# Turned tables in another order, a pooling weight and table copies begun elsewhere, and bias rows multiplied on TensorE, in a hybrid SSM and mixture-of-experts block

## The reference

```
mod = silu(c) @ w_mod + b_mod                       # six rows of 1024: shift, scale, gate, twice
hx  = rmsnorm(x, g_mix) * (1 + sc1) + sh1           # the same for ctx, with c_ctx's rows
ux  = hx @ w_in;   uc_ssm = hc @ w_in[:, 512:]
ssm  = S5 scan both ways (32 groups of 16 channels, 64 complex states), started from ctx's last state;
       gelu, then y * sigmoid(y @ w_glu + b_glu)
pool = (centred mean over 2/4/8/16 - u) @ w_pool[g] * s_pool      # four groups of 128 channels
x   = x + g1 * (concat(pool, ssm) @ w_out)
h2  = rmsnorm(x, g_ffn) * (1 + sc2) + sh2
experts, gates = group-limited top 2 of 32 by sigmoid(h2 @ w_router)
x   = x + g2 * sum(gate_e * (silu(h2 @ w_gate[e]) * (h2 @ w_up[e])) @ w_down[e])
out = rmsnorm(x, g_final)
```

## Time and profile before

| | |
|---|---|
| median of three runs | 665.77 us (665.63 to 666.22) |
| the profiled execution | 667.83 us |
| its span, first to last instruction | 665.7 us |
| busy in the span: TensorE / weight loads | 586.6 us (88%) / 248.5 us (37%) |
| busy: DVE / ScalarE / POOL | 201.5 (30%) / 149.4 (22%) / 57.5 us (9%) |
| moved by DMA | 248.99 MB, mean 374 GB/s |

### The profile page before, as it was taken

One profiled execution on the slowest core, in us unless ns is written; L12 is line 12 of the kernel. 1 busy time (PEld: TensorE's weight loads), 2 busy tenths in 40 slices (PEclk: granted clock), 3 DMA queues, 4 the chain that ended last, 5 costly groups with the idle time before them and its releaser, 6 DMA issues.

```text
span 665.7 us, 9385 instructions
## 1 busy us (share of the span) xinstructions
PE 586.6 (88%) x3770; PEld 248.5 (37%) x3770; DVE 201.5 (30%) x427; ACT 149.4 (22%) x239; POOL 57.5 (9%) x103
## 2 busy tenths in 40 slices
PE   1989995799789997899799979978997997899996
PEld 0454552465453333234233323423342342234331
DVE  7999388769850010002001000200110010002003
ACT  8472131031322212012111211221022112012111
POOL 4993000011300000000000000000000000000000
...
GB/s 314 421 401 89 253 244 333 292 412 389 378 278 420 423 420 422 422 421 423 420 423 419 422 421 422 423 420 423 422 423 420 423 421 421 423 421 366 402 207 64
DMA packets 47463, 248.99 MB, mean 374 GB/s; under 512 B 8888, under 2 KB 11592, under 8 KB 21072
## 3 DMA queue, kind: packets, MB, share of 16 engines
...
q0 software_dynamic: 352, 1.07, 0.7%
...
## 4 chain that ended last, share of the span: by engine, by line
PE 64%; DMA 24%; DVE 7%; issue 2%; ACT 1%; SPq 1%; DVEq 0%; POOL 0%; ACTq 0%
PE ps L847 21%; DMA wts<-in_w_up 21%; PE ps L887 17%; PE ps L817 5%; PE ps L823 5%; PE ps L609 4%; DVE rc L1168 3%; PE ps L699 2%; PE ps L622 2%; DMA ra<-in_w_pool 2%; DMA cb<-in_ssm_bc 1%; PE ps L642 1%; DVE ps L1168 1%; PE ps L512 1%; PE ps L863 1%
## 5 line engine op out<-in xcount | busy, mean ns | idle before, releaser
L847 PE MATMUL ps<-wts,ra 128*64 128x512 f32 x512 | 239.3, 619 | 36.1 <-DMA wts<-in_w_up 36.1
L848 PE MATMUL ps<-wts,ra 128*64 128x512 f32 x512 | 239.4, 620 | 0.0
L847 PEld LDWEIGHTS ps<-wts,ra 128*64 128x64 f32 x512 | 69.2, 142 | 179.5 <-issue 128.5
L887 PE MATMUL ps<-wts,ra 128*32 128x512 f32 x512 | 111.4, 593 | 0.0
L887 PE MATMUL ps<-rc,ra 128*32 128x512 f32 x512 | 111.4, 593 | 0.0
L1168 DVE TENSOR_TENSOR ra<-ra,ps 128x256 f32<-128x256 f32 x32 | 13.5, 422 | 270.6 <-ACT ra L1117 270.4
L1111 ACT COPY ra<-ps 128x512 f32<-128x512 f32 x32 | 33.5, 1048 | 211.6 <-PE ps L848 211.6
L848 PEld LDWEIGHTS ps<-wts,ra 128*64 128x64 f32 x512 | 69.2, 142 | 0.0
L887 PEld LDWEIGHTS ps<-wts,ra 128*32 128x32 f32 x512 | 29.2, 110 | 73.2 <-issue 73.2
L1168 DVE TENSOR_TENSOR cb<-ps,ra 128x512 f32<-128x512 f32 x32 | 22.2, 692 | 103.4 <-PE ps L887 103.4
L1106 ACT COPY ra<-ps 128x512 f32<-128x512 f32 x32 | 18.7, 585 | 140.8 <-PE ps L817 140.8
...
## 6 DMA issues: line engine op xcount, KB each, us to landing
...
```

The source lines that it names most:

```text
L847: pe.matmul(ps[0:64, 4 + b, :], st, Wg[b][:, k, :], start=(k == 0), stop=(k == KD - 1))
L848: mm = pe.matmul(ps[64:128, 4 + b, :], st, Wu[b][:, k, :], start=(k == 0), stop=(k == KD - 1))
L887: mm = pe.matmul(ps[32 * j:32 * j + 32, BANKS[n], :], hid[:, j, f, SLOTS * t:SLOTS * t + SLOTS], Wd[j][:, f, 512 * h:512 * h + 512], start ...
```

## The change

- TURNS: the table pieces are turned and laid out so that each half of the pairs of groups (h = 0, 1) lies together in ST; DVE builds its tables in the order SA_ORDER. Two pieces are no longer turned ahead of the first projection.
- w_in's SSM and pool columns lie in two separate halves of their place, so wo_ssm can be loaded once u_ssm is done.
- g_mix is the scale of `copy_xt`; A1 is gone. Steps k = 4 to 7 of the modulation of tokens are on DVE, as tensor_scalar.
- w_pool goes into the place of the powers `lam`, and is issued behind u8_in0's loads and three mod chunks.
- The first five Toeplitz copies are issued after state_inputs(0), the other ten after take_states(1). state_inputs(1) comes before all of u_pool.
- SyncE's order is changed for wo_ssm, wglu, "up" of expert 0, x, and the down weights.
- The bias rows are multiplied on TensorE (one partition of ones times the row) into the same PSUM banks; POOL's additions are gone. `start_outputs(1)` goes ahead of the gate product and the counts. POOL's memsets wait for passes_ready.
- One more of the gate's sums (four, not three) stands ahead of cat_ssm on DVE.

```
@@ -113,14 +113,15 @@
 wm0 = wm + [wts[:, 20480:22528], wts[:, 22528:24576], wts[:, 8192:10240], wts[:, 10240:12288], wm[0]]
-ST = wts[:, 4096:12288].rearrange("p (d r g m) -> p d r g m", d=2, r=2, g=GP)
-WB = wts[:, 12288:12288 + 8192].rearrange("p (k n) -> p k n", k=KD)
+ST = wts[:, 4096:12288].rearrange("p (h d r g m) -> p h d r g m", h=2, d=2, r=2, g=8)
+WBs = wts[:, 12288:16384].rearrange("p (k n) -> p k n", k=KD)
+WBp = wts[:, 16384:20480].rearrange("p (k n) -> p k n", k=KD)
 TT = wts[:, 4096:8192].rearrange("p (t n) -> p t n", t=L)
 tC, tD = ra[:, 3072:3328], ra[:, 3328:3584]
-wpool = ra[:, 5120:5632].rearrange("p (g n) -> p g n", g=4)
+wpool = lam[:, 0:512].rearrange("p (g n) -> p g n", g=4)
 wo_pool = wts[:, 8192:12288].rearrange("p (k n) -> p k n", k=4)
...
@@ -224,7 +224,8 @@
-TURNS = (0, 1, 2, 3, 4, 5, 10, 11, 6, 7, 12, 13, 8, 9, 14, 15)
+TURNS = (0, 1, 4, 5, 2, 3, 10, 11, 6, 7, 12, 13, 8, 9, 14, 15)
+SA_ORDER = ((0, 0), (1, 0), (0, 1), (1, 1))
...
@@ -305,7 +306,13 @@
             mod_chunk(1, k)
+        if h == 0:
+            sp.wait_ge(S("mo_powers"), 1)
+            sp.wait_ge(S("pw_ready"), 1)
+            sp.dma_start(wpool, w_pool[0].rearrange("g c d -> c g d")).then_inc(S("wpool_in"), 16)
+    sp.wait_ge(S("u_ssm_mm"), 4)
+    sp.dma_start(wo_ssm, w_out_v[:, 4:8, :]).then_inc(S("wo_ssm_in"), 16)
     sp.wait_ge(S("mod_used"), 14)
@@ -315,16 +322,17 @@
     sp.wait_ge(S("u_pool_mm"), NT)
-    sp.dma_start(wpool, w_pool[0].rearrange("g c d -> c g d")).then_inc(S("wpool_in"), 16)
+    sp.dma_start(wglu, w_glu[0].rearrange("(k p) n -> p k n", p=P)).then_inc(S("wglu_in"), 16)
+    sp.wait_ge(S("gff_row"), 16)
+    sp.dma_start(gffb, row_dram[1:2, 0:D].broadcast_to([P, D])).then_inc(S("gff_in"), 16)
+    sp.wait_ge(S("pool_mm"), 1)
+    last_third(3, 0)
     sp.wait_ge(S("mod1_row"), 16)
     sp.dma_start(sh2c, row_dram[0, D:2 * D].rearrange("(p k) -> p k", k=KD)).then_inc(S("sh2c_in"), 16)
-    sp.wait_ge(S("gff_row"), 16)
-    sp.dma_start(gffb, row_dram[1:2, 0:D].broadcast_to([P, D])).then_inc(S("gff_in"), 16)
-    sp.dma_start(wglu, w_glu[0].rearrange("(k p) n -> p k n", p=P)).then_inc(S("wglu_in"), 16)
-    sp.wait_ge(S("pool_mm"), 1)
-    last_third(3, 0)
-    sp.dma_start(wo_ssm, w_out_v[:, 4:8, :]).then_inc(S("wo_ssm_in"), 16)
+    sp.wait_ge(S("pool_mm"), 2)
+    gu_load(sp, 0, 0, 0, "up")
+    gu_load(sp, 0, 0, 1, "up")
@@ -332,26 +340,27 @@
         last_third(j, 1)
-    sp.wait_ge(S("y_mm"), 1)
-    for t in range(NT):
-        sp.dma_start(x2[:, t, :], x[0, t * P:(t + 1) * P]).then_inc(S(f"xres_in{t}"), 16)
-    gu_load(sp, 0, 0, 0, "up")
-    gu_load(sp, 0, 0, 1, "up")
+        if j == 2:
+            sp.wait_ge(S("y_mm"), 1)
+            for t in range(NT):
+                sp.dma_start(x2[:, t, :], x[0, t * P:(t + 1) * P]).then_inc(S(f"xres_in{t}"), 16)
+    down_load(sp, lambda j: j, 0, (3,))
     sp.wait_ge(S("mix_pool"), 1)
     gu_load(sp, 0, 0, 1, "gate")
-    down_load(sp, lambda j: j, 0, (3,))
     sp.wait_ge(S("mix_mm"), 4)
     down_load(sp, lambda j: j, 0, (2,))
+    sp.wait_ge(S("ss2_ready"), NT)
+    down_load(sp, lambda j: j, 1, (3,))
     sp.wait_ge(S("h2_rows"), 2 * NT)
-    down_load(sp, lambda j: j, 1, (2, 3))
+    down_load(sp, lambda j: j, 1, (2,))
@@ -464,18 +473,7 @@
     gp.dma_start(ctmp, w_router.rearrange("(p k) e -> p k e", k=KD)).then_inc(S("wr2_in"), 16)
-    def mod_bias(gate, done):
-        gp.wait_ge(S("mod2_used"), KD * gate + KD)
-        for n in range(2):
-            j = 2 * gate + n
-            a = acc[32 * j:32 * j + 1, 512 * j:512 * j + 512]
-            gp.tensor_tensor(a, a, modrow[32 * j:32 * j + 1, 2, :], ALU.add).then_inc(S(done), 1)
-            gp.wait_ge(S(done), n + 1)
-    gp.wait_ge(S("bmod_in"), 16)
-    mod_bias(0, "scale_sum")
-    mod_bias(1, "gate_sum")
+    gp.wait_ge(S("mod2_used"), 2 * KD)
     gp.dma_start(brb, b_router.rearrange("(a d) -> a d", a=1).broadcast_to([P, NE])).then_inc(S("br_in"), 16)
@@ -488,6 +486,7 @@
             gp.wait_ge(S("gate_mm"), 1)
+            gp.wait_ge(S("passes_ready"), 1)
             gp.memset(oS, 0.0).then_inc(S("zeroed"), 1)
@@ -524,8 +523,10 @@
         d, r, g4 = n // 8, n // 4 % 2, n % 4
-        if n < 10:
-            pe.wait_ge(S("sa_ready"), n // 2 + 1)
+        if n < 8:
+            pe.wait_ge(S("sa_ready"), SA_ORDER.index((r, g4 // 2)) + 1)
+        elif n < 10:
+            pe.wait_ge(S("sa_ready"), 5)
         else:
@@ -604,25 +605,26 @@
         for k in range(KD):
-            if q == 0:
+            if q == 0 and k < 4:
                 pe.wait_ge(S("ht_ready"), 2 * k + 2)
-            mm = pe.matmul(ps[:, 4 + q % 2, :], WB[:, k, 512 + P * q:512 + P * q + P], hT[:, k, :],
+            elif q == 0:
+                pe.wait_ge(S("ht_dve"), 2 * k - 6)
+            mm = pe.matmul(ps[:, 4 + q % 2, :], WBs[:, k, P * q:P * q + P], hT[:, k, :],
                            start=(k == 0), stop=(k == KD - 1))
-            if q == 0 and k in (1, 2):
-                turn_sa(11 + k)
-            elif q == 0 and k in (5, 6):
-                turn_sa(9 + k)
-            elif q == 1 and k == 1:
+            if q == 0 and k in (1, 2, 4, 5):
+                turn_sa(9 + k if k < 3 else 8 + k)
+            elif q == 1 and k in (0, 2):
+                turn_sa(14 + k // 2)
+            elif q == 1 and k == 5:
                 lag_kernels(1)
...
                     mm = pe.matmul(ps[64 * a:64 * a + 64, S_BANK[n % 3], 64 * g:64 * g + 64],
-                                   ST[:, d, r, gpair, 64 * a:64 * a + 64],
+                                   ST[:, h, d, r, g, 64 * a:64 * a + 64],
                                    U8[:, grp % 8, grp // 8].rearrange("p h c -> p (h c)"),
     lag_kernels(0)
-    turn_sa(10)
-    turn_sa(11)
     pe.wait_ge(S("win_ssm_in"), 16)
@@ -661,13 +661,12 @@
         mod_chunk(1, k, 6)
+    state_inputs(1)
+    for k in range(6, KD):
+        mod_chunk(1, k, 6)
     pe.wait_ge(S("kt_ready"), 2)
     pe.wait_ge(S("win_pool_in"), 16)
-    u_pool(0, range(0, 4))
-    state_inputs(1)
-    u_pool(0, range(4, KD))
-    for k in range(6, KD):
-        mod_chunk(1, k, 6)
+    u_pool(0)
     u_pool(1)
@@ -690,8 +689,9 @@
             grp = 8 * q + g
-            pe.matmul(ps[32 * q:32 * q + 32, 4 + g % 2, 128 * (g // 2):128 * (g // 2) + 128], U8[:, g, q, 1, :],
-                      TT[:, :, SG * grp:SG * grp + SG], start=(g < 2), stop=False, skip_group_check=True)
+            mm = pe.matmul(ps[32 * q:32 * q + 32, 4 + g % 2, 128 * (g // 2):128 * (g // 2) + 128], U8[:, g, q, 1, :],
+                           TT[:, :, SG * grp:SG * grp + SG], start=(g < 2), stop=False, skip_group_check=True)
+    mm.then_inc(S("pool_mm"), 1)
@@ -742,11 +742,18 @@
     pe.matmul(ps[:, 6, 0:NE], ones, cpart, start=True, stop=True).then_inc(S("shift_mm"), 1)
-    pe.wait_ge(S("scale_sum"), 2)
+    def modulation(gate, h):
+        j = 2 * gate + h
+        pe.matmul(ps[:, 6 + h, :], ones[32 * j:32 * j + 1, :], modrow[32 * j:32 * j + 1, 2, :], start=True, stop=False)
+        return pe.matmul(ps[:, 6 + h, :], ones, acc[:, 512 * j:512 * j + 512], start=False, stop=True)
+    pe.wait_ge(S("mod2_used"), KD)
+    modulation(0, 1)
     pe.wait_ge(S("shift_copy"), 1)
-    for h in range(2):
-        mm = pe.matmul(ps[:, 6 + h, :], ones, acc[:, 512 * h:512 * h + 512], start=True, stop=True)
-    mm.then_inc(S("scale_mm"), 1)
+    modulation(0, 0).then_inc(S("scale_mm"), 1)
     def start_outputs(t):
@@ -793,10 +800,11 @@
-    pe.wait_ge(S("gate_sum"), 2)
-    for h in range(2):
-        mm = pe.matmul(ps[:, 6 + h, :], ones, acc[:, 1024 + 512 * h:1536 + 512 * h], start=True, stop=True)
-    mm.then_inc(S("gate_mm"), 1)
+    start_outputs(1)
+    pe.wait_ge(S("mod2_used"), 2 * KD)
+    pe.wait_ge(S("a2b_ready"), 1)
+    modulation(1, 0)
+    modulation(1, 1).then_inc(S("gate_mm"), 1)
@@ -804,7 +812,6 @@
               skip_group_check=True).then_inc(S("count_mm"), 1)
-    start_outputs(1)
...
         act.wait_ge(S("x_t"), k + 1)
-        act.copy(hT[:, k, :], ps[:, 5 + k % 2, :]).then_inc(S("xt_copy"), 1)
+        act.activation(hT[:, k, :], ps[:, 5 + k % 2, :], ACT.Copy, scale=vt[:, V_GM + k:V_GM + k + 1]).then_inc(S("xt_copy"), 1)
@@ -988,18 +995,18 @@
     mod_rows(0, 4)
+    copy_st(8)
     mod_columns(4)
     act.wait_ge(S("mod_col"), 2)
-    act.wait_ge(S("a1_ready"), 1)
-    for at in (8, 9):
-        copy_st(at)
-    for k in range(KD):
+    for k in range(4):
         for q in (1, 0):
             act.activation(hT[:, k, 256 * (1 - q):256 * (2 - q)], hT[:, k, 256 * (1 - q):256 * (2 - q)],
-                           ACT.Identity, bias=MC[:, 0, k, q:q + 1], scale=A1[:, k, q:q + 1]).then_inc(S("ht_ready"), 1)
-        if k in (0, 1, 3, 4):
-            copy_st(10 + (k + 1) // 2 if k < 3 else 9 + k)
+                           ACT.Identity, bias=MC[:, 0, k, q:q + 1], scale=MC[:, 1, k, q:q + 1]).then_inc(S("ht_ready"), 1)
+        if k != 1:
+            copy_st(9 + (k + 1) // 2)
+    for at in (12, 13):
```

(32 more changed lines are left out.)

16 lines of the change are left out of this document (7 added, 9 removed).

## The result

The changed kernel takes 661.33 us (median of 5 runs, 657.66 to 661.57); the kernel before takes 665.77 us. Ratio 0.9912, 95% interval 0.9891 to 0.9933. It is faster, as forecast, but by 4.4 us where the forecast said 15.0, and it lies outside the range of 648.0 to 657.5.

A forecast was written before the change was run, and what follows sets the result against it. The start of the expert-weight stream, set by M, bounds the kernel. Gains of 9.7 (readout), 0.8 (bias) and 5.1 (routing) with small terms put M at 178.5: gain 15.4, less 0.4 for loads, so 650.8 us; range 648.0 to 657.5.

The forecast's parts named there:

- M: Start of the first expert matmul, which frees buffers for the expert weights; forecast to go from 193.1 to 178.5 us.
- The start: Up to the state inputs: first projection matmul limited by w_in's landing, full clock; 3.9 us sooner, bounds 2.0 and 4.3.
- VectorE's eight pieces: Modulated tokens moved to DVE: pieces wait for GpSimd's table work, done by 45 us; counted 0, bounds 0 and 6.
- State inputs, then all of the pool projection: From state inputs to pool projection's end: early gain spent in idle time; 108.7 us, 1.0 later than before.
- rival 2: Idle time before state_inputs(1) costs more, through low clock and late reads: 4 us instead of 1; 654 us; chance 16%.
- w_pool, the Toeplitz copies, hp: Pool projection to state readout: w_pool's wait goes, copies and hp just in time; readout 123.4, gain 9.7 us.
- Rival 1: Ahead of the readout: Toeplitz copies take w_pool's place as the wait, gaining 2.7 us, not 9.7; 658 us; chance 14%.
- Bias rows on TensorE: Readout to first x2 row and its transposes: POOL's additions go, TensorE gets more instructions; net gain 0.8 us.
- Routing: Choice of experts up to M: memset waits, start_outputs(1) goes ahead of the counts; gain 5.1 us, bounds 2.5 and 5.5.
- rival 4: At M: loads, not M, set the expert-weight stream's start, losing 5 us; 656 us; chance 8%.
- Rival 5: Slower: gate sums wait for last_third(1,1) behind early loads if queues run at 217 GB/s; 673 us; chance 4%.
- how M becomes the end: From M to kernel end: the first freed load flows from M + 5.2, so gain is 193.9 - M.

The follow-up runs named there:

- e2: Changed kernel with all 15 Toeplitz copies issued behind take_states(1), as before the change; 665.47 us, ratio 1.0016.
- e0_after: The changed kernel as it is, timed again; 660.42 us, ratio 0.9931.
- e3: Changed kernel with a quarter of the pool projection put back ahead of state_inputs(1); 659.01 us, ratio 0.9902.
- e4: Changed kernel with both VectorE's earlier out_copy credit and the pool projection's quarter back ahead of state_inputs(1); 656.53 us, ratio 0.9861.
- e10: e4 with the bias additions also back on GpSimd; 656.05 us, ratio 0.9854.
- e5: Kernel before with only w_pool's place and load changed; 664.42 us, ratio 0.9979.
- e11: e10 with the two up loads of expert 0 also issued late; 656.12 us, ratio 0.9854.
- e12: e4 with the two up loads of expert 0 also issued late; 656.56 us, ratio 0.9858.
- e7: Changed kernel with the two up loads of expert 0 back behind the inputs of the residual; 660.12 us, ratio 0.9919.
- e8: e4 with the first five Toeplitz copies issued by SyncE behind the eight reads, not by ScalarE beside them; 657.00 us, ratio 0.9873.
- e6: Changed kernel with the two bias additions back on GpSimd and each modulation a single matmul; 660.57 us, ratio 0.9918.
- e1: Changed kernel with VectorE's out_copy credit given right behind passes_ready; 657.16 us, ratio 0.9881.
- e0b_after: The changed kernel as it is, once more; 660.57 us, ratio 0.9920.
- e13: e8 with the two up loads of expert 0 also issued late; 655.14 us, ratio 0.9849.

## Why the prediction was wrong, by its own steps

| step | forecast | trace after | miss, grown so far |
|---|---|---|---|
| first projection matmul | 39.5 | 39.32 | -0.2 |
| state inputs, first half | 76.0 | 76.23 | +0.2 |
| end of pool projection | 108.7 | 111.9 | +3.2 |
| readout | 123.4 | 126.73 | +3.3 |
| count | 174.5 | 179.49 | +5.0 |
| M | 178.5 | 185.83 | +7.3 |

(174.5 is the forecast's M less its own four terms behind the count, 0.6, 0.8, 2.0 and 0.6. Before, count to M took 7.16 us; with 0.6, 0.8 and 2.0 in its place and 1.6 us gained ahead of the count, the routing gain is 5.4 us, where the forecast wrote 5.1.)

*The start* was right: w_in's landing is the releaser (1.02 us of waiting), the clock stays full, the state inputs gain 3.7 us. So were VectorE's eight pieces: 5.83 us together, done at 43.8, 0.2 us of waiting of TensorE for them. The first took 1.46 us, to 39.43, and the second 2.52, to 41.9, each until just after a table product of GpSimd had ended (39.27 and 41.71); the shortest took 0.40. By the Trainium skill (SBUF — State Buffer, "Who interferes with whom") tensor_scalar in its two-port mode and GpSimd keep each other out; the trace agrees with these two pieces, and L1492 took 0.17 us once the memset waited for it, against 1.80. Of the forecast's own two coincidences only that one is a tensor_scalar; A1's product was a tensor_tensor.

*"State inputs, then all of the pool projection"* is the first step that failed. Forecast: 3.6 us idle, 0.6 for the copies beside the reads, 3.95 us of work. Trace: 5.88 us idle and 6.32 us of work. The copies cost 2.2 us there and not 0.6 (e2, without them, waits 3.74 and e0_after 5.92), and the clock fell in the idle time: 2.4 us. Chunk 7's 0.7 us were not spent; with 0.2 from the step before and 0.4 of small terms given back, 1.7 + 2.4 - 0.7 + 0.2 - 0.4 = 3.2. This is rival 2's mechanism, at nearly its size. I had given it 16% and summed the forecast as if the clock held.

*"w_pool, the Toeplitz copies, hp"* was right in its order: no wait for w_pool, none for the Toeplitz copies, readout 14.8 us after the pool projection (forecast 14.7). The copies themselves were later than the 110 of the forecast, hidden behind the late pool part: where that ends sooner, in e3, e4 and e10, the Toeplitz product waits for them until 114.1 to 116.2. Rival 1 did not come, but e2 and e5 show how near it stood: without the five early copies the wait for w_pool returns as 6.3 to 6.9 us for these. And hp was as close as forecast: it holds the readout by 1.2 to 2.1 us in e3, e4, e10, e11 and e12.

*"Bias rows on TensorE"*, the second failed step: from readout to count 52.8 us, forecast 51.1. The four pairs for the scale take 4.12 us (148.28 to 152.40) where the two products took 1.79 after a wait of 0.95, so 1.4 and not 0.5. The rest are stops of TensorE that the forecast has no term for, 1.12 us with 0.5 around them. They hang together with the early up loads, which I had counted only as bandwidth: with these late they are gone in e7 and e12. But with them early and the first copies moved, 0.39 and 0.58 us are left (e2, e8), and with them late 0.91 in e11; so the loads are not the only cause, and what a stop is stays open. The term on last_third(1,1) was not needed. Of the 2.17 us product beside GpSimd about 0.9 and not 1.1 us was waiting: products of that size take 1.22 to 1.32. No timed run shows a gain from mending this step (e6, e7).

*"Routing"*, the third: its gains came (no wait at the counts, 2.02 us for the gather; 3.62 in e0_after, hidden behind the credit), but from count to M it took 6.34 us and not 4.0. The first instruction of VectorE behind the credit, in the trace before:

```profile
192.84 0.42 DVE L1168 TENSOR_TENSOR cb<-cst,ut 128x256 f32<-128x256 f32 x1 [1.21 <-issue]
```

That is 0.2 us ahead of M, so the credit was no wait there; the forecast moved the gathers forward and left the credit where it was. I had subtracted 0.6 us for the register load as TensorE's. It was VectorE's register load that counted, together with the 2.7 us of work ahead of it. e1 gives 2.4 us of it back.

*The loads* held, as forecast: what TensorE waited for at M was the credit, so rival 4 fell. Rival 5 fell too; from 115 to 145 us the windows after run at 398 to 424 GB/s. One of the forecast's signs did not show, 420 GB/s from 184 us on: it is 315 and 329 from 185 to 195, as M, and with it the first freed buffer, came late.

*From profile to median.* The forecast's own rule, a gain of 193.9 - M, gives 8.1 us for M at 185.83, and the medians show 4.4. So 7.3 of the 10.6 us missed are M's; the other 3.3 fall to the step "how M becomes the end", which carried one profile of the kernel before over to its median. M came 7.2 us sooner and the span fell by 9.9: from M to the last down matmul 445.9 us instead of 448.5. Within one and the same kernel this stretch is 445.9 (after, e0_after) or 449.5 (e0b_after). In e0b_after TensorE starts the first expert at the low clock, and the first buffer that it frees is reloaded at M + 5.4 and not M + 3.7. Its window and SyncE's row:

```profile
185.00:190.00 5.00, 3.27 (x10) 0.71 0.81 291
```
```profile
192.11 0.33 SPq L243 DMA_DIRECT2D wts<-in_w_gate  x1
```

Those 1.7 us are then kept to the last group. Another 1.8 us arise there, most of them as waits for up weights, which the trace before has too (0.33 and 1.21 us) and those of after and e0_after have not:

```profile
622.96 0.62 PE L854 MATMUL ps<-wts,ra 128*64 128x512 f32 x1 [0.29 <-DMA wts<-in_w_up]
627.83 0.64 PE L854 MATMUL ps<-wts,ra 128*64 128x512 f32 x1 [1.22 <-DMA wts<-in_w_up]
```

What decides that was not found. The trace of before had the second delay, that of after neither; the other kernels here have 446.0 to 448.1 us in this stretch. So the 2.6 us are not shown to be a gain of the change. Nor are all of M's 7.2 us: the profiled execution of before is itself 2.1 us slower than its kernel's median. One profile each does not divide it further.

*What is left.* With the credit, the wait and the copies mended (e13) M is at 181.9, still 3.4 later than forecast. Of this 0.7 us stands at the readout, the rest between readout and count: the bias pairs, one stop of 0.63 us, and start_outputs(1) at 5.21 us and not 3.68 with a granted clock of 0.84 and 0.82 in the two windows around it. No kernel of these came to 650.8.
